# Three conditioning loads moved behind a later weight load, and two ScalarE steps exchanged, in the first turn of a two-layer mixer kernel

## The reference

```python
mod = jax.nn.silu(c) @ w_ada + b_ada
shift, scale, gate = jnp.split(mod, 3, axis=-1)
h = _rmsnorm(x, norm_pre) * (1.0 + scale[:, None, :]) + shift[:, None, :]
z = h @ w_in
...
o = jnp.concatenate([y_conv, y_ret], axis=-1) @ w_out
return x + gate[:, None, :] * _rmsnorm(o, norm_post)
```

## Time and profile before

| | |
|---|---|
| median of 3 runs | 1731.1 us (1730.53 to 1733.04) |
| the profiled execution, whole time | 1732.72 us |
| its span | 1730.9 us |
| PE busy | 1696.8 us, 98% |
| DVE busy | 1132.4 us, 65% |
| ACT busy | 730.8 us, 42% |
| loaded and stored | 414.62 MB, 240 GB/s over the span |
| DMA, slices 1 to 3 of 40 (0 to 130 us) | busy share 9 tenths or more, 342 to 383 GB/s |

### The profile page before, as it was taken

The page is one execution under the profiler, slowest core; times in us unless marked ns, Lnnn a source line. Parts: engine busy times, 40 slices in busy tenths (PEclk is TensorE's granted clock), DMA queues, the critical chain, the costliest instruction groups (busy, mean ns, idle before and its releaser), DMA issues. The chain is left out here.

```text
span 1730.9 us, 19019 instructions
## 1 busy us (share of the span) xinstructions
PE 1696.8 (98%) x7779; PEld 1384.2 (80%) x7779; DVE 1132.4 (65%) x1303; ACT 730.8 (42%) x832; POOL 38.9 (2%) x78
## 2 busy tenths in 40 slices
PE   6989999999999999999999999999999999999998
PEld 3567888887888888888878888888888888888886
DVE  2688766878787766677776445555545555467776
ACT  3344444443444444343354443444344444444332
POOL 4000000000000000000000000000000000000000
PEclk9999999999999999999999999999999999999999
DMA  9998645777878867777765555555555555568775
GB/s 342 382 383 313 195 154 193 263 277 269 296 269 290 290 225 244 267 279 279 283 228 170 177 194 194 170 185 188 194 176 194 188 184 173 186 235 298 284 279 190
DMA packets 227399, 414.62 MB, mean 240 GB/s; under 512 B 7520, under 2 KB 48880, under 8 KB 226544
## 3 DMA queue, kind: packets, MB, share of 16 engines
q1 hardware_dynamic: 225888, 408.97, 68.3%
q10 hardware_dynamic: 1424, 4.43, 0.6%
HBM read 411.28 MB, written 2.10 MB: 239 GB/s over the span
## 5 line engine op out<-in xcount | busy, mean ns | idle before, releaser
L770 DVE TENSOR_TENSOR w_lo<-stage,w_hi 128x1024 fp32r<-128x1024 f32 x574 | 693.0, 1223 | 507.8 <-ACT w_hi L572 505.5
L572 ACT CAST w_hi<-stage 128x1024 fp32r<-128x1024 f32 x574 | 595.9, 1051 | 941.6 <-PE Z L1196 596.9
L1194 PE MATMUL Z<-w_hi,H 128*128 128x512 f32 x1784 | 703.6, 394 | 10.3 <-DVE w_lo L770 6.5
L1196 PE MATMUL Z<-w_hi,H 128*128 128x512 f32 x1784 | 695.8, 390 | 0.0
L1195 PE MATMUL Z<-w_lo,H 128*128 128x512 f32 x1784 | 695.0, 390 | 0.0
L1194 PEld LDWEIGHTS Z<-w_hi,H 128*128 128x128 f32 x1784 | 335.4, 188 | 88.2 <-issue 10.4
L1196 PEld LDWEIGHTS Z<-w_hi,H 128*128 128x128 f32 x1784 | 335.3, 188 | 71.1
L1195 PEld LDWEIGHTS Z<-w_lo,H 128*128 128x128 f32 x1784 | 335.5, 188 | 67.6
L791 DVE SCALAR_TENSOR_TENSOR acc<-stage,c_silu,acc 128x512 f32<-128x512 f32 x240 | 180.2, 751 | 6.8
L1194 PE MATMUL Z<-w_hi,YC 128*128 128x512 f32 x256 | 102.2, 399 | 0.0
L1194 PE MATMUL Z<-w_hi,YR 128*128 128x512 f32 x256 | 100.6, 393 | 0.2
(11 more groups left out here) (149 smaller groups left out, 697.1 us busy)
## 6 DMA issues: line engine op xcount, KB each, us to landing
stage<-in_w_in SPq DMA_DIRECT2D x186, 1024.0 KB, 5.2
stage<-in_w_ada SPq DMA_DIRECT2D x64, 1024.0 KB, 7.5
stage<-in_w_out SPq DMA_DIRECT2D x64, 1024.0 KB, 7.4
stage<-in_w_in SPq DMA_DIRECT2D x74, 512.0 KB, 5.4
front_stage<-in_w_ada SPq DMA_DIRECT2D x32, 1024.0 KB, 11.6
xt<-in_x SPq DMA_DIRECT2D x2, 1024.0 KB, 6.4
dec<-decay SPq DMA_DIRECT2D x8, 256.0 KB, 5.7
rows<-in_b_ada ACTq DMA_DIRECT2D x2, 1024.0 KB, 7.9
```

What stands on the lines that cost most here:

```text
L572: N.copy(w_bufs(n, h)[0], stage[:, slot_of(n), 2 * h:2 * h + 2, :]).then_inc(s_hi, 1)
L770: V.tensor_tensor(lo, stage[:, slot_of(n), 2 * h:2 * h + 2, :], hi.bitcast(F32), ALU.subtract)\
L1194: T.matmul(z[:, i, :], hh, wh, start=ch.first and a == 0, stop=False)
L1196: ins = T.matmul(z[:, i, :], hl, wh, start=False, stop=stop)
```

## The change

The three loads (6, 0), (6, 1) and (6, 2) of the fourth group's scale row stood one each behind the weights of chunks 11, 12 and 13. They now stand together behind the weights of chunk 14, and (6, 3) and (7, 0), which stood there, stand behind those of chunk 15, (7, 1) and (7, 2) behind 16, (7, 3) behind 17. From chunk 18 on the table is as it was. PE and DVE do their work on a conditioning chunk in the chunk behind which it is loaded, so that moves along: row 6 is added on DVE in chunk 16 instead of 15, and transposed in chunk 17 instead of 16. The second part of the change exchanges two steps of ACT: `h_full` of the third group (in chunk 14) comes ahead of `x_scaled` of the fourth.

```diff
-FRONT_AFTER = [1, 1, 1, 1, 1, 1, 1] + [2, 1, 1, 1, 1, 1, 1] + [2, 1, 1, 1, 1, 1, 1] + [2, 1, 1, 1, 0, 0, 0]
+FRONT_AFTER = [1, 1, 1, 1, 1, 1, 1] + [2, 1, 1, 1, 0, 0, 0] + [3, 2, 2, 1, 1, 1, 1] + [2, 1, 1, 1, 0, 0, 0]
...
-FRONT_ROW = {2: 2, 4: 3, 8: 4, 11: 5, 15: 6, 18: 7, 22: 8, 25: 9}
-FRONT_SUM = {2: 2, 4: 3, 8: 4, 11: 5, 16: 6, 18: 7, 23: 8, 25: 9}
+FRONT_ROW = {2: 2, 4: 3, 8: 4, 11: 5, 16: 6, 18: 7, 22: 8, 25: 9}
+FRONT_SUM = {2: 2, 4: 3, 8: 4, 11: 5, 17: 6, 18: 7, 23: 8, 25: 9}
...
+                if n == FRONT_LATE:
+                    h_full(0, *FRONT_GROUPS[ch.g])
                 if n < FRONT and ch.b == 0 and ch.g < LAST_GROUP:
                     x_scaled(ch.g + 1)
-                if n == FRONT_LATE:
-                    h_full(0, *FRONT_GROUPS[ch.g])
```

## The result

| | before | changed |
|---|---|---|
| median | 1731.34 us, 15 runs (1730.53 to 1733.52) | 1735.69 us, 15 runs (1734.27 to 1737.21) |
| profiled execution, whole time | 1732.72 us | 1735.29 us |
| its span | 1730.9 us | 1733.5 us |

The ratio is 1.0022, 95% interval 1.0015 to 1.0029: 2.6 to 5.0 us slower, 3.8 by the ratio; the two medians of the table differ by 4.4. The forecast was 1734.2, 2.9 us over the median of before in this table, within a range of 1730.9 to 1737.2.

A forecast was written before the change was run, and what follows sets the result against it. PE, busy 98% of the span, was taken to bound the kernel, with 4.4 us of gaps to win. DVE's 4.2 us of lateness less 1.0 of cover gave +3.1 on 1731.1: 1734.2 us, range 1730.9 to 1737.2.

The forecast's parts named there:

- Parts 1 and 2: Chunks 11 to 14: moved loads start chunk 14 5.2 us earlier; the exchange on ACT costs 1.2, leaving 4.2.
- Part 3: (7, 0) waits for (6, 0)'s slot until 95.4; DMA engines run dry 4 to 5 us; DVE 4.2 late.
- the restart: After the dry queue, (7, 0) and the weights of chunk 16 land after 8.4 us, between 7.9 and 9.0.
- Its lower bound: For the restart: a lone 1 MB weight load's median 5.2 us, plus 2.7 for one behind it: 7.9.
- the cover: PE's smallest slack against DVE, 1.0 us at chunk 23; of DVE's 4.2 us some 3.1 reach PE.
- PE's lead at chunk 16: DVE's add for chunk 16 done at 107.3, before 107.79: PE's lead down to 0.5 us.
- The line of 0.2%: What this kernel's measurement tells from no change, 3.5 us; the forecast lies just inside.
- Rival 1: DMA engines don't run dry, weights of chunk 17 land at 106.4, PE keeps 2.5 to 3.3 us: 1728.2; chance 0.06.
- Rival 2: Dear restart (9.0 us) and a clock fall behind a PE gap, 1.6 us lost: 1736.4; chance 0.20.
- Rival 3: Cheap restart, DVE late by 1 to 2 us, PE's cover takes it: +0 to +1, 1731.6; chance 0.14.

The follow-up runs named there:

- x_first: The changed kernel with only the exchange on ACT undone (x scaled ahead of h again), loads still moved; median 1734.52 us, ratio to before 1.0004 to 1.0023.
- h_first_alone: The kernel before with only the exchange on ACT (h ahead of scaling x), all loads where they were; median 1731.77 us, ratio 1.0000.
- used_late: The changed kernel with PE using (6, 0), (6, 1) and (6, 2) behind chunk 15, one chunk later; median 1739.78 us.
- used_early: The changed kernel with PE using (6, 0) and (6, 1) behind chunk 13 instead of 14; median 1729.82 us, ratio to before 0.9987.
- w16_ahead: The changed kernel with (7, 0) loaded behind the weights of chunk 16 instead of those of chunk 15; median 1732.87 us.
- v81_on_pe: The changed kernel with (8, 1) multiplied by PE behind chunk 19 instead of by DVE; median 1735.38 us.

## Why the prediction was right

**Parts 1 and 2, right to some tenths.** Chunk 14 was forecast at 86.9 and came at 86.77; ga at 84.0, came at 83.64; the cast of the second half at 89.0, came at 88.63; the second half at 91.4, came at 91.06. PE's use of (6, 0), forecast at 94.3, came at 93.99. The DMA engines were to run dry for 4 to 5 us; in the windows they stood from about 92 to 96. The exchange was said to cost 1.2 us and nothing if made alone; x_first and h_first_alone show about 1 and 0.

**Part 3, right in kind, its terms somewhat small.** PE had used (6, 0) at 93.99 + 1.06 = 95.05 and (7, 0) was issued at once (forecast 95.4). From there to the weights of chunk 16 the prediction took 8.4 us; it was 8.0 (103.08). From those to the weights of chunk 17 it took 8.1 for 3 MB; it was 9.4 (112.47). Together 16.5 were forecast and 17.4 came, in x_first and used_late too (17.6 and 17.5, reckoned in the same way). This is the term that was mis-sized, the restart with the five loads behind it. At the rate of 2.7 us per MB the five take 13.5, so the restart itself costs 3.9. The prediction had gone by the landing of the second load, which doesn't carry the whole of that. Its lower bound was also read too freely: 5.2 us is the median of all 186 weight loads of that kind in the kernel, and the row doesn't say which of them were alone in the queue.

**DVE and the cover, right.** DVE was 4.75 us late (forecast 4.2: the mis-sized term was 0.9 more, the earlier release 0.3 less). It never recovered before chunk 23. PE's cover at chunk 23 was put at 1.03 us, and 4.75 - 3.72 is 1.03. PE's gaps stood ahead of chunks 16, 17, 18, 21 and 23, the places that were named. Only PE's lead at chunk 16, put at 0.5 us, was 1.2 (106.57 against 107.79), as the weights of chunk 16 landed 0.7 us earlier than forecast; it made no difference to the sum, since chunk 17 waited for DVE anyway.

**The whole.** +3.1 was forecast, +3.8 measured, by the ratio and by chunk 23 alike. The line of 0.2%, 3.5 us, runs between, and the interval of 2.6 to 5.0 us lies on both sides of it: whether the change costs more than 0.2% is not settled.

**Rivals.** Rival 1 (the lead survives) named its own condition, (6, 0) used by 91 us. used_early is that case: forecast 2.5 to 3.3 us faster, measured 2.4 by chunk 23 and 2.2 by the medians. Rival 2 put a slow clock behind a long PE gap at 1.6 us and said that the wait for DVE behind it would cover it. The changed kernel's one profile shows no such fall. x_first and w16_ahead show it behind the gap ahead of chunk 17, nearly all of it covered, and v81_on_pe too, with some 0.7 us left over at chunk 18; there the waits at chunks 21 and 23, which could have covered the rest, were gone. That the clock stayed full in the changed kernel was luck, since behind gaps of nearly the same length in the same place it fell in three kernels; but by x_first, a fall there would have cost only some tenths of a microsecond. Rival 3 (all cancels) is out: the interval begins at +2.6 us.

**What SP's wait held up.** SP waited 13.9 us at a conditioning load while the weights behind it weren't issued; w16_ahead, which only puts them ahead, has them land 7.6 us earlier. The Trainium skill ("DMA: Bandwidth & Descriptors", section on the anatomy of one DMA) says that a semaphore wait happens on the issuing sequencer, ahead of dispatch; this case's trace agrees. An estimate from the same section's fit, measured on another path, would have made the loss 2 to 3 us smaller; the landings, 5.4 us for 2 MB (112.47 to 117.89 in the changed kernel), say otherwise.

## What to carry to other kernels

Where a load and its use are tied to the same step, as here, moving the load later moves its use later as well, and the load that waits for its buffer with it; in a queue of one order this blocks all that stands behind, so look for the last use of the slot and not for the load. Where a ring of buffers feeds a full DMA queue, compare the time of that use with the time at which the backlog ends, here 95 against 92 us; a consumer that takes the buffer a little earlier can turn the loss into a gain (here +3.8 into -2.4 us, with two of PE's steps moved by one chunk, partly into a gap that PE had anyway). And an engine that is nearly full, like DVE here, hands every microsecond of a late start on, less the smallest cover that follows.

## What the runs showed of the hardware

- A queue that ran dry cost 3.9 to 4.1 us over the plain rate before the fifth load had landed (17.4 to 17.6 us for 5 MB in four kernels, at 2.7 us per MB), though the second landed after 8.0 to 8.2, 2.6 to 2.8 over its rate. With four loads behind the restart (w16_ahead) it was 14.6 us, 3.8 over the rate. Why part of the difference shows only further behind stays open.
- The granted clock behind a gap isn't settled by the gap's length alone: gaps of 2.76 (x_first), 2.50 (v81_on_pe) and 2.46 us (w16_ahead) ahead of chunk 17 were followed by half the clock, 2.66 us at the same place in the changed kernel by full clock. In the kernel before, 1.92 us ahead of chunk 8 was followed by half the clock and 2.29 us ahead of chunk 14 wasn't. What tells these apart stays open.
